# Recurrent pairs of an RWKV-7 block on one core: the state step as two 64x64 products instead of one block-diagonal 128x128 product

## The chip, the cores and the metric

The kernel runs on one core of one Trainium2 chip. The metric is the device time of one execution in microseconds (us). Matrix products run on TensorE (PE, its weight loads PEld), elementwise work on VectorE (DVE) and ScalarE (ACT), the low halves of the weights on GpSimd (POOL), and SyncE (SP) issues most transfers. All data is fp32; the sequence has 512 tokens, and the width is 1024.

## What is computed

The reference is a block that holds an RWKV-7 recurrence, dilated attention, a cross attention and an FFN, followed by two layers of another block (Fourier mixing, retention, convolutional FFN). Only the recurrence is touched. It has 16 heads, each with a state of 64 x 64:

```python
def step(state, inp):
    r_t, w_t, k_t, v_t, a_t, b_t = inp
    sa = jnp.einsum('bhij,bhj->bhi', state, a_t)
    state = state * w_t[:, :, None, :] + sa[..., None] * b_t[:, :, None, :] + v_t[..., None] * k_t[:, :, None, :]
    return state, jnp.einsum('bhij,bhj->bhi', state, r_t)
```

## The kernel before

**Layout.** The kernel does not step token by token. It cuts the 512 tokens into 8 chunks of 64 (`NC = 8`, `CH = 64`) and treats two heads at a time (`PAIRS = 8`): one head of a pair lies in partitions 0 to 63, the other in 64 to 127 (`HALVES`). Within a chunk everything is turned into small products, and from chunk to chunk a 64 x 64 state is carried per head: state(c+1) = decay x (map(c) applied to state(c)) + new part(c). The map of a chunk is the identity plus a 64 x 64 product, kept in `MCX`. In `MCX` each chunk has 128 columns: the upper head's 64 x 64 map in rows 0 to 63 and columns 0 to 63, the lower head's in rows 64 to 127 and columns 64 to 127, and zeros in the other two quarters. One product with all 128 rows then steps both heads.

**Order on PE.** The order is written out by hand in the body of `for p in range(PAIRS)`. Each pair issues some thirty groups of products (`to_tokens`, L1254; `to_heads`, L1265; both work on 64 x 64 quarters of the array, all four quarters in turn). Between them stand pieces of other matrix products (`pieces(n)`): one piece is one 128-row block of a projection and is three products of 128x512, L906, L907 and L910 (high x high, high x low, low x high). Near the end of a pair stand the groups `N` and `RM`, two pieces, then the scan:

```python
b = start_group("scan", p)
pe.wait_ge(sem("rw_mcx"), p + 1)
scan_step(b, 1)
pieces(1)
scan_step(b, 2)
```

and so on to `scan_step(b, 6)`, after which `values_inside` (L1298, L1301: quarter products in the two diagonal quarters) follows without a piece between. So a pair has six state steps, and five of them stand between two pieces. A state step is at L1435 (one product, 128x128 stationary `MCX[:, c, :]`, 64 moving columns); from the second on it waits for the state before it. An fp32 product of this kind, L1435 as L1298, shows as two MATMUL records and two weight loads; the transposes at L1273 as one.

**Order on DVE.** When `RM` is made, DVE writes the maps (`state_map`, L3066) once for each head, 64 partitions at a time, the second of which releases `rw_mcx`. Then it makes state 2 (`scanned(1)`, L3075), adds a term to x (L3147), and makes states 3 to 7, with work for the next pair in between (L2955, L2935, L2939). At the start of the kernel it clears `MCX` once (L2816).

Of the kernel before, what the change touches and what calls it, by code (L numbers as in the profile page):

```python
# [16 lines left out]
P = 128  # L17
F32 = mybir.dt.float32
F32R = mybir.dt.float32r
ALU = mybir.AluOpType  # L20
# [8 lines left out]
CH = 64  # L29
NC = S // CH  # L30
# [240 lines left out]
def build_program(nc, plan, ap, out):  # L271
# [4 lines left out]
    for t, T in enumerate(tiles):  # L276
        for i, (u, _, _) in enumerate(T["blocks"]):
            last_block[u] = (t, i)
# [12 lines left out]
    with ctx:  # L291
# [5 lines left out]
        def sem(name):  # L297
            if name not in sems:
                sems[name] = ctx.enter_context(nc.semaphore(name))
            return sems[name]  # L300
# [30 lines left out]
        def take(*shape):  # L331

            n = 1
            for x in shape:
                n *= x
            a = arena[:, free_at[0]:free_at[0] + n]
            free_at[0] += n
            assert free_at[0] <= ARENA, (free_at[0], ARENA)
            if len(shape) == 2:
                return a.rearrange("p (a b) -> p a b", b=shape[1])  # L340
            if len(shape) == 3:
                return a.rearrange("p (a b c) -> p a b c", b=shape[1], c=shape[2])
            return a

        def prm(name, j=0, n=1):
            return params[:, PCOL[name][0] + j:PCOL[name][0] + j + n]

        def tab(name):
            return table[:, TCOL[name][0]:TCOL[name][1]]

        ident, ones, heads, centring, strict, incl, ident_c, reset, quads = (
            tab(n) for n in ("ident", "ones", "heads", "centre", "strict", "incl", "ident_c", "reset", "quads"))
# [32 lines left out]
        main_arena = arena  # L385
        arena, free_at[0] = arena2, 0
        AR1 = take(NC, 2, CH)
        MCX = take(NC, P)
        BK, KK_, NP_, SC_ = (take(NC, CH) for _ in range(4))
        free_at[0] = 5 * KT * S // 4 + 3 * S  # L390
        YT, YSQ, BO1 = (take(S) for _ in range(3))
# [165 lines left out]
        def units_until(end):  # L557

            at = {}
            for j, t in enumerate(NOW[0] + NOW[1]):  # L560
                for i, (u, _, _) in enumerate(tiles[t]["blocks"]):
                    at[u] = KT * j + i
            return max([min(at)] + [u + RING for u in at if at[u] <= end])
# [55 lines left out]
        def emptied(eng, name, p):  # L619

            e, n = EMPTIED[name, p]
            eng.wait_ge(sem("rw_emptied_" + e), n)

        def made(eng, name, p):

            early = 1 if name == "aB" and p else 0
            late = 1 if name == "Y" and p + 1 < PAIRS else 0
            eng.wait_ge(sem("rw_made"), STEP_NO[name, p] + 1 - early + late)
# [5 lines left out]
        def in_columns(name, p, w):  # L634

            return slot_of(name, p)[:, :, 0:4 * w].rearrange("p b (d s) -> p b d s", s=w)
# [5 lines left out]
        def by_head(x):  # L642

            return x.rearrange("p (d r) s -> p r d s", r=2)

        HALVES = slice(0, CH), slice(CH, P)

        def state(c):

            return SC_[:, c, :] if c > 1 else NP_[:, 0, :]  # L650
# [23 lines left out]
        def rsqrt(n):  # L674

            return stats[:, n % 2, :]
# [103 lines left out]
        @block.sync  # L780
        def _(sp):
            first_up = min(u for u, _, _ in tiles[stages["up0"][0]]["blocks"])
            for u in range(n_units):
                n = u - first_up - 3 - ADA_LATE
# [79 lines left out]
        def _(pe):  # L864
# [377 lines left out]
            def start_group(name, p):  # L1242
                n = STEP_NO[name, p] - 2
                if n >= 0:
                    emptied(pe, *STEP_AT[n])
                return slot_of(name, p)
# [148 lines left out]
            for p in range(PAIRS):  # L1395
# [33 lines left out]
                def scan_step(b, c):  # L1429

                    if c == 1:
                        emptied(pe, "N", p)
                    else:
                        pe.wait_ge(sem("rw_state"), p * (NC - 3) + c - 1)
                    mm = nc.tensor.matmul(b[:, 0, CH * c:CH * (c + 1)], MCX[:, c, :], state(c), start=True, stop=True)  # L1435
                    mm.then_inc(sem("rw_made" if c == NC - 2 else "rw_stepped"), 1)

                if p == 0:
# [79 lines left out]
# [6 lines that stand above are left out]
                scan_step(b, 3)  # L1524
                pieces(1)
                scan_step(b, 4)
# [63 lines left out]
            for hd in range(XH):  # L1590
# [6 lines left out]
                for c in range(TC):  # L1597
                    for n, (k, (a, b)) in enumerate(itertools.product(range(2), HI_LO)):
                        mm = nc.tensor.matmul(banks[4 + c // 2][:, M * (c % 2):M * (c % 2 + 1)],
                                              XQS[a][:, (2 * hd + k) % 4, c * P:(c + 1) * P], KMS[b][:, 2 * hd + k, :],  # L1600
                                              start=(n == 0), stop=(n == 5))
# [13 lines left out]
                for m in range(2):  # L1615
                    for c in range(TC):
                        mm = nc.tensor.transpose(banks[6 + m][:, c * P:(c + 1) * P], XP[:, c, m * P:(m + 1) * P], ident)
# [6 lines left out]
                for d in range(2):  # L1624
                    for n, (m, (a, b)) in enumerate(itertools.product(range(2), HI_LO)):
                        mm = nc.tensor.matmul(banks[6 + d][:], VMS[a][:, m, 256 * hd + P * d:256 * hd + P * (d + 1)],
                                              XPTS[b][:, m, :], start=(n == 0), stop=(n == 5))
# [46 lines left out]
            for l in range(LAYERS):  # L1674
# [85 lines left out]
                for hd in range(XH):  # L1760
# [3 lines left out]
                    for c in range(TC):  # L1764
# [3 lines left out]
                        for k in range(2):  # L1768
# [3 lines left out]
                            mm = nc.tensor.matmul(o, RK_LO[:, k, cols], RQ_HI[:, k, :], start=False, stop=(k == 1))  # L1772
# [8 lines left out]
                    for d in range(2):  # L1781
                        for c in range(TC):
# [3 lines left out]
                            mm = nc.tensor.matmul(o, RV_LO[:, c, cols], high, start=False, stop=(c == TC - 1))  # L1786
# [7 lines left out]
                    for c in range(TC):  # L1794
                        mm = nc.tensor.matmul(banks[5][:, c:c + 1], ROT[:, 2, c * P:(c + 1) * P], ones[:, 0:1], start=True,
                                              stop=True)
# [24 lines left out]
            for c in range(TC // 2):  # L1821
                mm = nc.tensor.transpose(banks[6][:, c * P:(c + 1) * P],
                                         rsqrt(len(REQUESTS) - 1)[:, c:c + 1].to_broadcast([P, P]), ident)
# [741 lines left out]
        def _(dve):  # L2565
            counts = {}
            V_ = nc.vector

            def do(ins, signal="vector_step", value=None):

                if value is None:
                    value = counts[signal] = counts.get(signal, 0) + 1
                ins.then_inc(sem(signal), 1)
                dve.wait_ge(sem(signal), value)
# [238 lines left out]
            do(V_.tensor_scalar(half_k_a, prm("k_a", 0, KT), 0.5, None, ALU.mult))  # L2813
            do(V_.tensor_scalar(rest_k_a, half_k_a, -1.0, 1.0, ALU.mult, ALU.add))
            do(V_.tensor_scalar(half_bias, prm("w0", 0, 16), 0.5, None, ALU.mult), "rw_zeroed")
            do(V_.memset(MCX, 0.0))  # L2816

            def difference(t, i):
                evacuated(dve, t)
# [42 lines left out]
            for it in range(2 * TC):  # L2862
                m, c = it // TC, it % TC
# [29 lines left out]
            def mask(m):  # L2893
                return m.unsqueeze(1).unsqueeze(1).to_broadcast([P, 2, 4, CH])
# [140 lines left out]
            for p in range(PAIRS):  # L3035
# [26 lines left out]
                rm = in_columns("RM", p, P)  # L3062
                x = by_head(AR[:, :, 1, :])

                def state_map(r, signal="vector_step"):
                    do(V_.tensor_tensor(by_head(MCX[r, :, r]), rm[r, :, :, CH:P], mask(ident_c)[r], ALU.add), signal)  # L3066

                def scanned(c):

                    last = c == NC - 2  # L3070
                    if last:
                        made(dve, "scan", p)
                    else:
                        dve.wait_ge(sem("rw_stepped"), p * (NC - 3) + c)
                    do(V_.scalar_tensor_tensor(state(c + 1), slot_of("scan", p)[:, 0, CH * c:CH * (c + 1)],  # L3075
                                               w_end[:, c:c + 1], NP_[:, c, :], ALU.mult, ALU.add),
                       "rw_emptied_v" if last else "rw_state")
# [58 lines left out]
                if more:  # L3136
# [4 lines left out]
                                    w_end.rearrange("p (d r) -> p r d", r=2).unsqueeze(3).to_broadcast([P, 2, 4, CH]),  # L3141
                                    ALU.mult), "rw_emptied_v")
                made(dve, "RM", p)
                state_map(HALVES[0])
                state_map(HALVES[1], "rw_mcx")
                scanned(1)
                do(V_.tensor_tensor(x, x, rm[:, :, :, 0:CH], ALU.add), "rw_emptied_v")  # L3147
                scanned(2)
# [209 lines left out]
            for l in range(LAYERS):  # L3358
# [109 lines left out]
                rows = slice(64, 96)  # L3468
# [300 lines left out]
```

## Time and profile before

| | before |
|---|---|
| median of 3 runs | 2911.92 us (2911.47 to 2911.98) |
| the profiled execution | span 2909.9 us, of which the median lies 2.0 us above |
| PE busy | 2892.3 us, 99% of the span |
| DVE / ACT / POOL busy | 54% / 38% / 54% |
| state steps L1435 | 48 products (96 records), 241 to 563 us |
| map writes L3066 | 16 x 0.69 us |

The page gives no other time of the profiled execution than its span; the 2.0 us between the two lie around the span. The pairs run from about 206 to 565 us of the span. In the timelines the first column is the start of a row in us from the start of the span, the second its length, and xN is the number of records merged into the row. The start of one row to the start of the next is the time that PE spends on it; the lengths overlap.

### The profile page before, as it was taken

What the parts mean: (1) busy time and instruction counts of PE and PEld (TensorE: products, weight loads), DVE (VectorE), ACT (ScalarE), POOL (GpSimd) and SP (SyncE); (2) the same over time, 40 slices, a digit from 0 to 9 for tenths busy, and PEclk for the clock granted to TensorE, in tenths of its full rate; (3) what the DMA queues carried; (4) which work ended last, traced back from release to release, by engine and by line L of the source; (5) the groups of instructions that cost most, each with busy time, mean ns of one, the idle gap of its engine ahead of it and who ended that gap; (6) DMA issues with size and microseconds to landing.
All of it is one profiled execution on the core that took longest, in us unless ns stands there. A gap on an engine that the chain in (4) does not pass through costs nothing.

```text
span 2909.9 us, 49401 instructions
## 1 busy us (share of the span) xinstructions
PE 2892.3 (99%) x19658; PEld 2423.8 (83%) x19658; DVE 1572.7 (54%) x2227; ACT 1103.5 (38%) x1673; POOL 1584.3 (54%) x1912
## 2 busy tenths in 40 slices
PE   9999999999999999999999999999999999999998
PEld 7877777788888888888888898888898888988887
DVE  5467877524556666775334265445763441473635
ACT  4454434333443322443433343233443342342323
POOL 6432233355646666677444557565584444565654
PEclk9999999999999999999999999999999999999999
DMA  5211111332426777533222323232333222232232
GB/s 173 94 45 41 42 55 45 97 141 95 130 82 217 252 273 254 179 113 126 85 89 73 95 87 113 87 109 87 106 124 115 77 88 87 87 102 94 94 102 73
DMA packets 92292, 322.21 MB, mean 111 GB/s; under 512 B 10144, under 2 KB 14368, under 8 KB 91808
## 3 DMA queue, kind: packets, MB, share of 16 engines
q1 hardware_dynamic: 84544, 302.39, 31.7%
q10 hardware_dynamic: 7520, 16.67, 1.7%
q8 instruction: 156, 2.56, 0.4%
q14 instruction: 72, 0.59, 0.1%
HBM read 315.09 MB, written 3.93 MB: 110 GB/s over the span
## 4 chain that ended last, share of the span: by engine, by line
PE 98%; issue 1%; DVE 1%; POOL 1%; DMA 0%; ACT 0%; POOLq 0%; SPq 0%; ACTq 0%; DVEq 0%
PE bank L906 25%; PE bank L910 25%; PE bank L907 25%; PE bank L1254 2%; PE bank L899 2%; PE bank L901 2%; PE bank L900 2%; PE bank L1265 2%; PE bank L1273 1%; PE bank L934 1%; PE bank L936 1%; PE bank L935 1%; PE bank L958 1%; PE bank L960 1%; PE bank L1785 1%
## 5 line engine op out<-in xcount | busy, mean ns | idle before, releaser
L837 POOL TENSOR_TENSOR w_lo<-w_raw,w_hi 128x256 fp32r<-128x256 f32 x1736 | 1419.2, 852 | 986.9 <-ACT w_hi L1862 980.5
L906 PE MATMUL bank<-act,w_hi 128*128 128x512 f32 (+1 forms) x3464 | 1312.7, 379 | 4.7 <-POOL w_lo L837 2.6
L910 PE MATMUL bank<-act,w_lo 128*128 128x512 f32 (+1 forms) x3464 | 1292.4, 373 | 0.0
L907 PE MATMUL bank<-act,w_hi 128*128 128x512 f32 (+1 forms) x3464 | 1291.4, 373 | 0.0
L906 PEld LDWEIGHTS bank<-act,w_hi 128*128 128x128 f32 x3464 | 652.9, 188 | 126.1 <-issue 8.3
L910 PEld LDWEIGHTS bank<-act,w_lo 128*128 128x128 f32 x3464 | 652.6, 188 | 115.2
L907 PEld LDWEIGHTS bank<-act,w_hi 128*128 128x128 f32 x3464 | 653.4, 189 | 106.7
L1862 ACT CAST w_hi<-w_raw 128x1024 fp32r<-128x1024 f32 (+1 forms) x438 | 454.4, 1043 | 345.1 <-DMA w_raw<-in_weights 163.6
L1870 ACT ACTIVATE arena<-bank 128x512 f32<-128x512 f32 (+1 forms) x177 | 104.3, 593 | 418.2 <-PE bank L910 401.6
L855 POOL TENSOR_TENSOR stats<-stats,exponent 128x8 f32<-128x8 f32 (+2 forms) x38 | 46.6, 1226 | 302.5 <-DVE stats L2914 150.0
L2600 DVE TENSOR_TENSOR act<-tmp,act 128x512 fp32r<-128x512 f32 (+1 forms) x140 | 121.2, 866 | 77.3 <-ACT act L1889 72.7
L3588 DVE TENSOR_SCALAR arena<-arena,params 128x512 f32<-128x512 f32 x88 | 53.0, 602 | 172.3 <-ACT arena L1870 171.9
L3323 DVE SCALAR_TENSOR_TENSOR arena<-arena,small 128x1024 f32<-128x1024 f32 x93 | 136.5, 1468 | 3.3
L837 POOL TENSOR_TENSOR w_lo<-arena,w_hi 128x256 fp32r<-128x256 f32 x128 | 114.9, 932 | 22.5 <-ACT w_hi L1862 22.5
L1889 ACT CAST act<-tmp 128x512 fp32r<-128x512 f32 (+1 forms) x140 | 84.4, 605 | 112.5 <-DVE tmp L3212 32.0
L2773 DVE SCALAR_TENSOR_TENSOR arena<-bank,small,arena 128x512 f32<-128x512 f32 x48 | 36.1, 751 | 166.9 <-PE bank L910 166.6
L2125 ACT ACTIVATE arena<-bank 128x512 f32<-128x512 f32 (+1 forms) x104 | 64.8, 631 | 114.3 <-PE bank L1273 96.9
L899 PE MATMUL bank<-w_hi,act 128*128 128x512 f32 (+1 forms) x224 | 84.5, 377 | 0.0
L3591 DVE SCALAR_TENSOR_TENSOR arena<-arena,params 128x512 f32<-128x512 f32 x88 | 82.6, 939 | 3.1
L901 PE MATMUL bank<-w_hi,act 128*128 128x512 f32 (+1 forms) x224 | 83.7, 374 | 0.0
L900 PE MATMUL bank<-w_lo,act 128*128 128x512 f32 (+1 forms) x224 | 83.7, 374 | 0.0
L2771 DVE TENSOR_TENSOR arena<-arena,bank 128x512 f32<-128x512 f32 x44 | 30.3, 688 | 89.5 <-PE bank L910 89.2
(359 smaller groups left out, 3087.4 us busy)
## 6 DMA issues: line engine op xcount, KB each, us to landing
w_raw<-in_weights SPq DMA_DIRECT2D x471, 512.0 KB, 3.5
arena<-in_ada SPq DMA_DIRECT2D x96, 512.0 KB, 5.0
arena<-in_strips ACTq DMA_DIRECT2D x8, 448.0 KB, 3.7
arena<-in_x ACTq DMA_DIRECT2D x1, 2048.0 KB, 10.9
y_scratch<-tmp ACTq DMA_DIRECT2D x7, 256.0 KB, 2.0
arena<-y_scratch ACTq DMA_DIRECT2D x1, 1792.0 KB, 8.1
arena<-in_dft ACTq DMA_DIRECT2D x2, 777.5 KB, 4.2
arena<-in_x SPq DMA_DIRECT2D x3, 512.0 KB, 7.4
```

Source lines behind the costliest of these rows:

```text
L837: ins = nc.gpsimd.tensor_tensor(w_lo[:, k, cols], weights_of(u)[:, cols], w_hi[:, k, cols].bitcast(F32), ALU.subtract)
L899: nc.tensor.matmul(o, xs[0], wh, start=first, stop=False)
L900: nc.tensor.matmul(o, xs[0], wl, start=False, stop=False)
L901: mm = nc.tensor.matmul(o, xs[1], wh, start=False, stop=last)
L906: nc.tensor.matmul(o, wh, xh, start=first, stop=False)
L907: nc.tensor.matmul(o, wh, xl, start=False, stop=False)
L910: mm = nc.tensor.matmul(o, wl, xh, start=False, stop=last)
L1862: nc.scalar.copy(x, y).then_inc(sem("w_high"), 1)
L1870: nc.scalar.activation(dst, banks[bank_of(t)][:, 0:n], func, scale=scale).then_inc(sem(f"bank_free{bank_of(t)}"), 1)
L1889: ins = nc.scalar.copy(o, x) if shift is None else nc.scalar.activation(o, x, ACT.Identity, bias=shift)
L2600: do(V_.tensor_tensor(o, x, h, ALU.subtract), "low_done")
L3323: do(V_.scalar_tensor_tensor(o, w, c_act[:, k:k + 1], o, ALU.mult, ALU.add), "ada_used")
```

## The change

`MCX` keeps only the two 64 x 64 maps, one above the other (64 columns to a chunk; the other half of the space is left unused, so that nothing behind it moves). A state step becomes two products, each 64 x 64 with 64 moving columns: rows 0 to 63 into output partitions 0 to 63, rows 64 to 127 into output partitions 64 to 127. DVE writes both maps with one operation over 128 partitions instead of two over 64, and the clearing at the start goes.

```diff
-        MCX = take(NC, P)
+        MCX = take(NC, CH)
+        take(NC * CH)
...
-                    mm = nc.tensor.matmul(b[:, 0, CH * c:CH * (c + 1)], MCX[:, c, :], state(c), start=True, stop=True)
+                    for rows in HALVES:
+                        mm = nc.tensor.matmul(b[rows, 0, CH * c:CH * (c + 1)], MCX[rows, c, :], state(c)[rows], start=True,
+                                              stop=True)
                     mm.then_inc(sem("rw_made" if c == NC - 2 else "rw_stepped"), 1)
...
-            do(V_.memset(MCX, 0.0))
...
-                def state_map(r, signal="vector_step"):
-                    do(V_.tensor_tensor(by_head(MCX[r, :, r]), rm[r, :, :, CH:P], mask(ident_c)[r], ALU.add), signal)
+                def state_map():
+                    do(V_.tensor_tensor(by_head(MCX), rm[:, :, :, CH:P], mask(ident_c), ALU.add), "rw_mcx")
...
-                state_map(HALVES[0])
-                state_map(HALVES[1], "rw_mcx")
+                state_map()
```

Line numbers shift by one or two in the changed kernel (L906, L907, L910 are L907, L908, L911 there, L1435 is L1437, L3066 is L3068).

On PE, at the last two state steps of the first pair, before the change:

```order
1357 L910 MATMUL bank<-act,w_lo 128x512
1358 L1435 MATMUL bank<-arena 128x64
1359 L906 MATMUL bank<-act,w_hi 128x512
1360 L907 MATMUL bank<-act,w_hi 128x512
1361 L910 MATMUL bank<-act,w_lo 128x512
1362 L1435 MATMUL bank<-arena 128x64
1363 L1298 MATMUL bank<-arena 64x64 x2
```

and now:

```order
1357 L911 MATMUL bank<-act,w_lo 128x512
1358 L1437 MATMUL bank<-arena 64x64 x2
1359 L907 MATMUL bank<-act,w_hi 128x512
1360 L908 MATMUL bank<-act,w_hi 128x512
1361 L911 MATMUL bank<-act,w_lo 128x512
1362 L1437 MATMUL bank<-arena 64x64 x2
1363 L1299 MATMUL bank<-arena 64x64 x2
```

The place of the step between the pieces is the same; one whole-array product has become two quarter products.

On DVE, where the first pair's maps are written, before the change:

```order
141 L3140 TENSOR_TENSOR arena<-bank,small 128x2x4x64
142 L3066 TENSOR_TENSOR arena<-bank,table 64x2x4x64 x2
143 L3075 SCALAR_TENSOR_TENSOR arena<-bank,small,arena 128x64
144 L3147 TENSOR_TENSOR arena<-arena,bank 128x2x4x64
145 L3075 SCALAR_TENSOR_TENSOR arena<-bank,small,arena 128x64
```

and now:

```order
140 L3142 TENSOR_TENSOR arena<-bank,small 128x2x4x64
141 L3068 TENSOR_TENSOR arena<-bank,table 128x2x4x64
142 L3077 SCALAR_TENSOR_TENSOR arena<-bank,small,arena 128x64
143 L3148 TENSOR_TENSOR arena<-arena,bank 128x2x4x64
144 L3077 SCALAR_TENSOR_TENSOR arena<-bank,small,arena 128x64
```

Two operations over 64 partitions have become one over 128, and nothing else on DVE changes its place.

## Rows read from the trace of the kernel before

**Rows 1.** The page: busy time of each engine, and the chain that ended last.

```profile
PE 2892.3 (99%) x19658; PEld 2423.8 (83%) x19658; DVE 1572.7 (54%) x2227; ACT 1103.5 (38%) x1673; POOL 1584.3 (54%) x1912
...
PE 98%; issue 1%; DVE 1%; POOL 1%; DMA 0%; ACT 0%; POOLq 0%; SPq 0%; ACTq 0%; DVEq 0%
```

**Rows 2.** Windows: stretch, its length, busy us of PE, PEld, DVE, ACT, POOL, clock.

```profile
284.97:290.60 5.63, 5.58 (x33) 4.16 (x33) 4.06 (x11) 0.00 (x0) 0.97 (x2) 1.00 0.47 160
557.29:562.90 5.61, 5.56 (x33) 4.16 (x33) 2.44 (x7) 0.00 (x0) 2.91 (x5) 1.00 0.59 184
565.00:1200.00 635.00, 635.00 (x3014) 532.53 (x3015) 347.49 (x427) 228.01 (x330) 387.05 (x455) 1.00 0.54 183
```

**Rows 3.** Timeline of PE, second pair: first, second and sixth state step.

```profile
284.97 0.40 PE L910 MATMUL bank<-act,w_lo 128*128 128x512 f32 x1
285.42 0.41 PE L1435 MATMUL bank<-arena 128*128 128x64 f32 x2
285.63 0.48 PE L906 MATMUL bank<-act,w_hi 128*128 128x512 f32 x1
285.95 0.40 PE L907 MATMUL bank<-act,w_hi 128*128 128x512 f32 x1
286.18 0.40 PE L910 MATMUL bank<-act,w_lo 128*128 128x512 f32 x1
286.42 0.33 PE L1435 MATMUL bank<-arena 128*128 128x64 f32 x2
286.56 0.48 PE L906 MATMUL bank<-act,w_hi 128*128 128x512 f32 x1
286.87 0.39 PE L907 MATMUL bank<-act,w_hi 128*128 128x512 f32 x1
...
290.18 0.33 PE L1435 MATMUL bank<-arena 128*128 128x64 f32 x2
290.44 0.33 PE L1298 MATMUL bank<-arena 64*64 64x64 f32 x4
290.60 0.28 PE L1301 MATMUL bank<-arena 64*64 64x64 f32 x4
290.72 0.28 PE L1298 MATMUL bank<-arena 64*64 64x64 f32 x4
```

**Rows 4.** Timeline of PE: a group on quarters between two pieces.

```profile
258.96 0.40 PE L910 MATMUL bank<-act,w_lo 128*128 128x512 f32 x1
259.29 0.69 PE L1265 MATMUL bank<-arena 64*64 64x64 f32 x32
259.92 0.50 PE L906 MATMUL bank<-act,w_hi 128*128 128x512 f32 x1
260.25 0.40 PE L907 MATMUL bank<-act,w_hi 128*128 128x512 f32 x1
```

**Rows 5.** Waits of PE's weight loads: us in total, times, longest.

```profile
PEld bank L1435 <- issue: 3.7, 8, 0.5
PEld bank L1435 <- DVE arena L3075: 2.6, 10, 0.4
```

**Rows 6.** Timeline of DVE, second pair, around its scan.

```profile
283.91 1.41 DVE L3066 TENSOR_TENSOR arena<-bank,table 64x512 f32<-64x512 f32 x2 [0.18 <-PE bank L1265]
...
285.93 0.28 DVE L3075 SCALAR_TENSOR_TENSOR arena<-bank,small,arena 128x64 f32<-128x64 f32 x1 [0.61 <-PE bank L1435]
286.25 0.69 DVE L3147 TENSOR_TENSOR arena<-arena,bank 128x512 f32<-128x512 f32 x1
...
290.01 0.69 DVE L2939 SCALAR_TENSOR_TENSOR arena<-arena 128x512 f32<-128x512 f32 x1
...
290.74 0.28 DVE L3075 SCALAR_TENSOR_TENSOR arena<-bank,small,arena 128x64 f32<-128x64 f32 x1
```

**Rows 7.** Timeline of DVE: the clearing at the start, and what follows it.

```profile
51.47 0.91 DVE L2816 MEMSET arena<- 128x1024 f32 x1 [0.28 <-DVE small L2815]
68.67 1.89 DVE L2874 SCALAR_TENSOR_TENSOR arena<-arena,bank 128x128 f32<-128x128 f32 x6 [16.28 <-PE bank L1182]
```

## The prediction

> **What bounds the kernel now.** The page comes first: PE is busy for 99% of the span, and 98% of the chain that ended last is PE [rows 1]. So a change counts by what it does to the time between PE's instructions, and work taken from DVE counts only where PE waits for it. The windows come next: behind the pairs lie 635 us in which PE has no gap at all [rows 2], so what the pairs gain or lose is not absorbed there. Then the timeline of PE at the state steps, because the change sits there, and the waits of its weight loads. I read starts, not lengths: a row's length holds the way through the array, which overlaps with the next row.
>
> **A state step now.** Take the second one of the pair [rows 3]: L910 to L1435 0.24 us, L1435 to L906 0.14, L906 to L907 0.31, L907 to L910 0.23 (285.95 to 286.18). That is 0.92 us for a step and a piece. A piece alone costs three times 0.23, 0.69, so an undisturbed step costs 0.23. Six steps, five with a piece, and the way into the quarter products (0.24, then 290.18 to 290.44, then to 290.60: 0.26 and 0.16) make 5 x 0.92 + 0.66 = 5.26 us. The window from the L910 before the first step to the first L1301 is 5.63 us in this pair and 5.61 in the last [rows 2]; the missing 0.37 are waits. At the first step PE comes 0.45 behind L910 instead of 0.24, and the next row 0.21 instead of 0.14 behind it: 0.28 us. The rest, 0.09, is at steps that wait for the state before them. Over the eight pairs the waits view shows both: 8 waits before the first step and 10 for L3075 [rows 5]. It names the first kind "issue", but DVE says what it is: the two map writes take until 285.32, and the load starts right behind [rows 6].
>
> **What the change does on DVE.** One write over 128 partitions instead of two over 64. An operation on 128x512 that also reads a bank, L3147, takes 0.69 us, and the two 64x512 writes take 1.41 together [rows 6]: length goes by the elements in a partition, so one write costs 0.69. The maps are ready at 283.91 + 0.69 = 284.60, before PE even starts the L910 at 284.97, so the wait at the first step goes in all eight pairs. The later waits go too: DVE is 0.7 us earlier, and PE comes later (below). Gain: 0.37 us in a pair, 3.0 in all. The clearing (0.91 us) is followed by 16.28 us of idle DVE [rows 7]; it was hidden by that and brings nothing.
>
> **What it does on PE.** The step becomes a small group on quarters of the array between two whole-array pieces. The trace has such groups, only larger [rows 4]:
> - L910 to the first quarter record: 0.33 us, against 0.24 to a whole-array step. The load does not run ahead beside L910.
> - first quarter record to the next L906: 0.63 for 32 records whose last one ends 0.69 after the start; so L906 starts 0.06 before the end of the group. For two products (4 records) in the two diagonal quarters, behind a whole-array product, the row at 290.44 is exactly the case: 0.33 long [rows 3]. So 0.33 - 0.06 = 0.27, against 0.14.
> - L906 to L907: 0.33 (259.92 to 260.25), against 0.31; I take 0.33 to 0.34. L907 to L910: 0.23 as before.
>
> Sum: 0.33 + 0.27 + 0.34 + 0.23 = 1.17 us for a step and a piece, 0.25 more than 0.92. The sixth step is followed by quarters anyway: 0.33 in, then 0.16 to L1298 (the gap behind a first pair of products), then 0.12 as from 290.60 to 290.72: 0.61 against 0.66. A pair thus needs 5 x 1.17 + 0.61 = 6.46 us against 5.63, +0.83, of which the waits that go are already taken off. Eight pairs: +6.6 us. On the profiled span that is 2909.9 to 2916.5; on the median, which is 2.0 above it, 2918.5.
>
> The unknown is the gap of 0.27. Its lower bound is the whole-array step's own 0.14 (then a pair's sum is 0.65 less, +1.4 us in all), its upper bound the 0.63 of the large group (+21 us). I stay near 0.27 because the row of 0.33 has the same four records; the 0.63 holds eight times as many.
>
> Here a rule of the Trainium skill bears on the case. In "TensorEngine Tiling (Array Packing)", Key Properties, it says that changing the tiling mode, and not only the tile, drains TensorE; it speaks against this change, which adds ten such changes to a pair, and the trace agrees with 0.33 against 0.24. The same page's Theoretical Speedup promises up to twice the rate where a dimension is 64 or less; by that alone the 48 steps would cost half of 0.23 each and the sum would be a gain of 5.5 us, 8.5 with the waits. Which of the two decides hangs on how many products share one change of mode: sixteen in the groups of the trace, two here.
>
> **What is late next.** DVE starts a state 0.10 after its product ends (285.83 to 285.93) [rows 3, 6]. With a step every 1.17 us, the next product is made 1.17 later, while DVE needs 0.28 for the state, 0.69 for the longest work between (L2939) and some 0.1 of gaps: 1.1 us. So no new wait for the state, with 0.1 to spare. At the sixth step DVE then starts 0.33 + 0.10 behind it, 0.15 behind the first L1301, where it is 0.14 now: what follows keeps its distance.
>
> **Rivals.**
> - *Price of leaving the quarters is hidden* (not slower). L906's weights are loaded while the four small records run, as they are behind a whole-array step: gaps 0.33, 0.16, 0.31, 0.23 = 1.03. A pair is 5 x 1.03 + 0.61 = 5.76, +0.13, in all +1 us: 2913. For it: a pair leaves half of the array untouched, and four records are few. Against it: each quarter group that is followed by a piece has L906 to L907 at 0.33, which shows the load uncovered. It decides if the gap behind a pair is under 0.2.
> - *No price for the change of mode at all* (faster). Gaps 0.23, 0.12, 0.23, 0.23 = 0.81; with the sixth step at 0.23 + 0.12 + 0.12 a pair takes 4.5, -1.1, in all -9 us: 2903. The rule of the speedup in the Trainium skill (same page) would have it so. Against it: no quarter group between pieces in the trace shows 0.23 on its way in.
> - *The two products don't run side by side* (slower still). If L906 has to wait for two pair gaps rather than one, 0.12 more a step: 40 x 0.12 = 4.8 on top, 2923. For it: an isolated pair has no later products to fill the array. Against it: the row of 0.33 is already the whole pair.
> - *The order on PE hides another wait.* That DVE's 0.7 us come back elsewhere would give at most 5.6 us; against it, DVE's next state is tied to PE's step, so DVE cannot run ahead. I count it with the first rival.
>
> **How the numbers follow.** A measurement of this kernel can tell about 0.2%, 5.8 us, from no change. Forecast, both changes of mode paid: 0.70, with its own range of +4.5 to +9 us, three quarters of it above 5.8. Price of leaving hidden, with little lost or gained: 0.14. No price: 0.06. Not side by side: 0.10. Slower by over 0.2%: 0.54 + 0.10 = 0.64; within: 0.16 + 0.14 = 0.30; faster: 0.06. The range reaches from the first rival to the third, and leaves out the fast case and the tails: 2912.5 to 2923.0.
>
> **What the profile after should show.** L1437 with 192 records on 64*64; the wait "issue" before it gone as a wait for DVE, though a gap behind L911 may bear that name; DVE L3068 eight times at 0.69; from L911 to L1437 0.33 at every step, the first like the others; from L1437 to L907 0.27; from L907 to L908 0.34; the window from the L911 before the first step to the first L1302 at 6.46 us in every pair; 635 us of a PE without gaps unchanged behind. I am wrong if that window is under 6.2 or over 6.8 us, or if PE's gaps change outside the eight windows.

## The result, and the profile after

The changed kernel takes 2918.41 us in the median of 12 runs (2917.88 to 2920.05), the kernel before, beside it, 2911.85 us (2911.47 to 2912.72). The ratio is 1.0023, with an interval from 1.0016 to 1.0030: slower by 6.6 us, where 2918.5 was forecast. The profiled execution has a span of 2916.5 us, against 2909.9.

The page of the changed kernel, busy time by engine, answers to [rows 1]:

```profile
PE 2897.9 (99%) x19754; PEld 2418.5 (83%) x19754; DVE 1565.4 (54%) x2218; ACT 1103.5 (38%) x1673; POOL 1578.6 (54%) x1912
```

PE is busy for 5.6 us longer and has 96 records more (48 steps with four instead of two). Its weight loads are busy for less time: a load of 64 columns takes 0.13 us instead of 0.19, and the loads of the two quarters overlap. DVE has nine instructions and 7.3 us less. Neither saving of busy time shortens the span by itself, because the span follows the starts of PE's products; what the earlier maps save is measured below (two_writes).

The window that the sum was made for, from the L911 before the first step to the first L1302, of the second and of the last pair (same columns as [rows 2]):

```profile
285.67:292.06 6.39, 6.39 (x45) 3.69 (x45) 3.80 (x10) 0.00 (x0) 0.96 (x2) 1.00 0.37 126
562.75:569.12 6.37, 6.37 (x46) 3.69 (x46) 2.10 (x6) 0.00 (x0) 2.92 (x5) 1.00 0.49 167
```

6.39 us instead of 5.63, and PE is busy for all of it. The eight windows add up to 51.17 us, against 45.25 before. The timeline of PE in the second pair, to be laid beside [rows 3]:

```profile
285.67 0.39 PE L911 MATMUL bank<-act,w_lo 128*128 128x512 f32 x1
285.99 0.33 PE L1437 MATMUL bank<-arena 64*64 64x64 f32 x4
286.25 0.50 PE L907 MATMUL bank<-act,w_hi 128*128 128x512 f32 x1
286.58 0.39 PE L908 MATMUL bank<-act,w_hi 128*128 128x512 f32 x1
286.81 0.40 PE L911 MATMUL bank<-act,w_lo 128*128 128x512 f32 x1
287.14 0.33 PE L1437 MATMUL bank<-arena 64*64 64x64 f32 x4
287.40 0.50 PE L907 MATMUL bank<-act,w_hi 128*128 128x512 f32 x1
287.74 0.39 PE L908 MATMUL bank<-act,w_hi 128*128 128x512 f32 x1
...
291.78 0.33 PE L1437 MATMUL bank<-arena 64*64 64x64 f32 x4
291.94 0.28 PE L1299 MATMUL bank<-arena 64*64 64x64 f32 x4
292.06 0.28 PE L1302 MATMUL bank<-arena 64*64 64x64 f32 x4
```

From L911 to the step 0.32 to 0.33 us, to the next L907 0.26, to L908 0.33 to 0.34, to L911 0.23: 1.15 to 1.16 us for a step and a piece, at the first step as at the others. The sixth step takes 0.16 to L1299.

The waits view of the changed kernel, between 180 and 600 us, names something that the prediction had ruled out:

```profile
PEld bank L1437 <- DVE arena L3077: 14.6, 40, 0.4
...
PEld bank L1437 <- issue: 2.9, 8, 0.4
```

L3077 is the state step on DVE. Read at face value, 40 of the 48 steps wait for the state before them, 14.6 us in all, five times what stood there before [rows 5]. DVE's timeline, though, has the state done early (second pair):

```profile
284.60 0.69 DVE L3068 TENSOR_TENSOR arena<-bank,table 128x512 f32<-128x512 f32 x1 [0.18 <-PE bank L1266]
286.43 0.28 DVE L3077 SCALAR_TENSOR_TENSOR arena<-bank,small,arena 128x64 f32<-128x64 f32 x1 [1.14 <-PE bank L1437]
```

The maps are ready at 285.29, before the L911 at 285.67; state 2 is ready at 286.71, before the L911 at 286.81, and the step comes at 287.14. Whether the waits view or this reading is right is the first question for the experiments.

### The profile page after: what moved, and what is told of

Read it like the earlier page. It is cut to its first block, busy times and chain, and to the rows that moved or that the text cites. A ratio compares the mean times of both kernels' runs of the same rounds, so it can differ in the third digit from the quotient of the medians.

```text
span 2916.5 us, 49584 instructions
## 1 busy us (share of the span) xinstructions
PE 2897.9 (99%) x19754; PEld 2418.5 (83%) x19754; DVE 1565.4 (54%) x2218; ACT 1103.5 (38%) x1673; POOL 1578.6 (54%) x1912
## 4 chain that ended last, share of the span: by engine, by line
PE 97%; issue 1%; POOL 1%; DVE 1%; DMA 0%; ACT 0%; POOLq 0%; SPq 0%; ACTq 0%; DVEq 0%
PE bank L907 26%; PE bank L908 25%; PE bank L911 25%; PE bank L1255 2%; PE bank L900 2%; PE bank L902 2%; PE bank L901 2%; PE bank L1266 2%; PE bank L1274 1%; PE bank L935 1%; PE bank L937 1%; PE bank L936 1%; PE bank L959 1%; PE bank L961 1%; PE bank L1788 1%
## 5 line engine op out<-in xcount | busy, mean ns | idle before, releaser
L907 PE MATMUL bank<-act,w_hi 128*128 128x512 f32 (+1 forms) x3464 | 1313.1, 379 | 5.1 <-POOL w_lo L838 2.8
L911 PE MATMUL bank<-act,w_lo 128*128 128x512 f32 (+1 forms) x3464 | 1291.9, 373 | 0.0
L908 PE MATMUL bank<-act,w_hi 128*128 128x512 f32 (+1 forms) x3464 | 1290.9, 373 | 0.4 <-issue 0.4
L907 PEld LDWEIGHTS bank<-act,w_hi 128*128 128x128 f32 x3464 | 652.2, 188 | 130.0 <-issue 8.9
L911 PEld LDWEIGHTS bank<-act,w_lo 128*128 128x128 f32 x3464 | 652.2, 188 | 116.2 <-issue 0.6
L908 PEld LDWEIGHTS bank<-act,w_hi 128*128 128x128 f32 x3464 | 652.8, 188 | 106.2
```

The lines of the kernel that those rows point to most:

```text
L907: nc.tensor.matmul(o, wh, xh, start=first, stop=False)
L908: nc.tensor.matmul(o, wh, xl, start=False, stop=False)
L911: mm = nc.tensor.matmul(o, wl, xh, start=False, stop=last)
```

## The experiments

All runs are against the kernel before on the same chip. "Window" is the stretch of the second pair as above (from the row ahead of its first step to the first row of the second line of `values_inside`), "sum" that of all eight pairs, both taken from starts in the timeline of the one profiled execution.

| kernel | window | sum | median us | before, same chip |
|---|---|---|---|---|
| before | 5.63 | 45.25 | | 2911.8 to 2912.1 |
| after | 6.39 | 51.17 | 2918.41 | 2911.85 |
| one_write | 5.33 | 42.67 | 2909.18 | 2911.81 |
| two_writes | 6.52 | 52.10 | 2918.76 | 2911.81 |
| free_state | 6.41 | 51.12 | 2918.86 | 2911.81 |
| doubled | 7.09 | 56.63 | 2923.58 | 2911.81 |
| one_product | 6.26 | 50.08 | 2917.59 | 2912.01 |
| column_halves | 6.66 | 53.32 | 2919.82 | 2912.01 |
| six_maps | 5.37 | 42.90 | 2909.74 | 2912.01 |
| six_maps_mixed | 5.52 | 44.26 | 2911.28 | 2912.01 |
| halved_sum | 5.32 | 42.97 | 2909.95 | 2911.91 |
| halved_sum_mixed | 5.26 | 42.57 | 2909.69 | 2911.91 |
| third_piece | 5.33 | 42.66 | 2912.36 | 2912.14 |

Median less sum lies between 2866.5 and 2867.7 us for all but third_piece (2869.7), which moves work out of the window. So the medians follow the windows within some 1 us, and what is said of differences under 1 us rests on the windows. The 95% intervals of the ratios reach about 0.1%, some 2.6 us, to either side. The medians of the kernels that come out 2 to 2.6 us under the kernel before are therefore not clear of no change by these intervals; that they save rests on the windows, and on times that don't overlap with those before (one_write 2908.69 to 2909.49 against 2911.36 to 2913.18; halved_sum's times do overlap).

**Each part by itself: one_write and two_writes.** The first keeps the whole-array step and writes the maps with one operation:

```diff
-                state_map(HALVES[0])
-                state_map(HALVES[1], "rw_mcx")
+                do(V_.tensor_tensor(by_head(MCX[:, :, 0:CH]), rm[:, :, :, CH:P], mask(ident_c), ALU.add), "rw_mcx")
```

> The whole-array step of the kernel before, but both maps written by one operation over 128 partitions into columns 0 to 63 of MCX, so that the lower head's map stands in the wrong columns (its state is not the reference's); only the DVE part of the change. Theory (the change = waits removed, -3.0 us, plus two changes of tiling mode at each isolated step, +9.1 us): this run shows the first term alone. Window from the L910 before the first step to the first L1301 5.26 to 5.30 us instead of 5.63, span 2.6 to 3.0 us under before. Rival (DVE is in lockstep with PE and the earlier maps bring nothing, the wait only moves to the next step): window 5.6, span unchanged. Second rival (the clock or the waits elsewhere carry the difference): the window changes, but the span by another amount than eight times it.

Measured: window 5.33 instead of 5.63, median 2.6 us under before. The first term stands, though 0.52 of the 2.58 us of the sum come from the seventh pair alone, which was longer than the others before (last section). The 0.03 to 0.07 us more than expected are one wait that stays: the third step's, one in each pair:

```profile
PEld bank L1435 <- DVE arena L3075: 2.0, 8, 0.3
```

The addition to x (0.69 us) stands between DVE's first and second state and makes the second late. I had thought that DVE's lead would carry over; it doesn't, since DVE's first state waits for PE's first step.

The second writes the maps twice, on 64 partitions each, in the changed kernel:

```diff
-                def state_map():
-                    do(V_.tensor_tensor(by_head(MCX), rm[:, :, :, CH:P], mask(ident_c), ALU.add), "rw_mcx")
+                def state_map(r, signal="vector_step"):
+                    do(V_.tensor_tensor(by_head(MCX[r]), rm[r, :, :, CH:P], mask(ident_c)[r], ALU.add), signal)
```

> The changed kernel with the two 64-partition map writes of before: only the PE part of the change, the output is the same. Theory: the steps cost what they cost in the changed kernel (1.155 us for a step and a piece), and the first step waits for the maps again, but little, since on quarters PE comes only 0.33 behind L911 in any case and the second write ends 0.35 behind it: 0.1 us a pair, so 0.8 to 1.0 us over the changed kernel. With one_write this makes the parts add up: after - before = +6.6 = (-3) + (+9.5). Rival (the maps' wait costs as much as before, 0.28): 2.3 us over the changed kernel.

Measured: window 6.52, 0.13 more than the changed kernel, 0.9 us over the eight pairs as expected; the median shows 0.35 of it. So the one write is worth 0.30 us a pair to whole-array steps and 0.12 to quarter steps (0.93 over eight pairs). Taken alone, the PE part costs 52.10 - 45.25 = 6.9 us, and the DVE part gives back 0.9 of it. The two parts don't add: most of the wait that the DVE part removes would have been hidden behind the drain that the PE part brings.

**Is it the state that PE waits for: free_state.**

```diff
-                    else:
-                        pe.wait_ge(sem("rw_state"), p * (NC - 3) + c - 1)
...
-                        mm = nc.tensor.matmul(b[rows, 0, CH * c:CH * (c + 1)], MCX[rows, c, :], state(c)[rows], start=True,
+                        mm = nc.tensor.matmul(b[rows, 0, CH * c:CH * (c + 1)], MCX[rows, c, :], NP_[rows, 0, :], start=True,
...
-                    do(V_.scalar_tensor_tensor(state(c + 1), slot_of("scan", p)[:, 0, CH * c:CH * (c + 1)],
+                    do(V_.scalar_tensor_tensor(state(c + 1), NP_[:, c, :],
```

> The changed kernel with the recurrence cut: every step reads NP_[:, 0] instead of the state before it and doesn't wait for it, and DVE makes its states from NP_ alone and not from the scan's bank (the recurrence is left out, the output is not the reference's). The number and the place of all instructions stay. Rival (the waits view of the changed kernel is right: 40 waits of PE's weight loads for L3077, 14.6 us): the span falls by up to 14.6 us. Theory (DVE had the state 0.1 us before L911 even started; what lies between L911 and the step is the change of tiling mode, and the view puts it down to the semaphore that came last): no change of the span beyond 0.5 us, step and piece still 1.155 us, L911 to the step still 0.33.

Measured: 2918.86 us, sum of the windows 51.12 against 51.17. No step waits for a state any more, and nothing is gained. The waits view of this run (the step is L1435 here):

```profile
PEld bank L1435 <- issue: 17.4, 48, 0.4
```

17.4 us at 48 steps, where the changed kernel has 14.6 + 2.9 = 17.5 at 40 + 8. The gap is the same to 0.1 us; only its name has changed. It belongs to the change of tiling mode, not to the state. The view puts a gap down to the last semaphore event ahead of it, and that was DVE's state, which had come 0.1 us before L911 even began.

**What the price hangs on: doubled and one_product.** `for rows in HALVES` becomes `for rows in HALVES * 2` in the one, and in the other

```diff
-                    for rows in HALVES:
+                    for rows in HALVES[:1]:
```

> The changed kernel with each step's two products issued twice, to the same place: 8 records instead of 4. Theory (a fixed price for going into the quarters and back, and 0.12 us for each pair of products within): a step and a piece 1.27 us instead of 1.155, 48 x 0.12 = 5.6 us over the changed kernel. Rival (isolated products on quarters don't overlap, and each pays its own way through the array): 0.2 us or more for each pair of products, 10 us or more over the changed kernel. Rival (the products are free beside the change of mode): under 2 us.

> The changed kernel with only the upper head's product in each step (the lower head's recurrence is left out, its states come from what the bank holds). 2 records instead of 4. Doubling the products cost 0.114 us a pair of products. Theory (side by side: the two products run in two quarters at once, and what takes 0.11 is the two passes of each, one after the other in its quarter): leaving one product out saves nothing, a step and a piece 1.15 us, under 0.6 us in all. Rival (in order: each product takes 0.057 whatever its quarter): a step and a piece 1.10 us, 48 x 0.057 = 2.7 us under the changed kernel. In both the price of going in and out, some 0.3 us, stays; if that went with the product (a step under 1.0 us), the change of mode would not be what costs.

Measured, second pair, doubled first:

```profile
286.23 0.40 PE L911 MATMUL bank<-act,w_lo 128*128 128x512 f32 x1
286.56 0.45 PE L1437 MATMUL bank<-arena 64*64 64x64 f32 x8
286.94 0.50 PE L907 MATMUL bank<-act,w_hi 128*128 128x512 f32 x1
287.27 0.40 PE L908 MATMUL bank<-act,w_hi 128*128 128x512 f32 x1
```

and one_product:

```profile
285.81 0.40 PE L911 MATMUL bank<-act,w_lo 128*128 128x512 f32 x1
286.13 0.33 PE L1437 MATMUL bank<-arena 64*64 64x64 f32 x2
286.39 0.50 PE L907 MATMUL bank<-act,w_hi 128*128 128x512 f32 x1
...
291.90 0.27 PE L1437 MATMUL bank<-arena 64*64 64x64 f32 x1
291.91 0.27 PE L1299 MATMUL bank<-arena 64*64 64x64 f32 x1
```

The way in (0.32 to 0.33) and the way out to L908 (0.33) are the same in both. From the step to L907 it is 0.38 us with four products, 0.26 with two and 0.26 with one. So a second pair costs 0.12 us (5.2 us in the median over the changed kernel), and the second product of the first pair costs nothing at an isolated step: the two quarters do work at once. Record by record the trace says the same: in the changed kernel the four records of the first step start at 285.986, 285.992, 286.092 and 286.098, and the two of one_product 0.107 us apart. So the second product starts 0.006 us behind the first, beside it, and only the second record of each has to wait for its first. The saving of one_product, 0.8 us in the median and 1.1 in the sum, is more than the 0.6 that were expected at most. Nearly all of it comes from the sixth step, where its last rows show L1299 starting 0.01 us behind it, beside it in the array, and not 0.16. The side-by-side theory holds, and with it the rival of a pair that doesn't run side by side is out.

**Is it the cut by rows: column_halves.** The kernel before, with the step cut by columns only:

```diff
-                    mm = nc.tensor.matmul(b[:, 0, CH * c:CH * (c + 1)], MCX[:, c, :], state(c), start=True, stop=True)
+                    for rows in HALVES:
+                        mm = nc.tensor.matmul(b[rows, 0, CH * c:CH * (c + 1)], MCX[:, c, rows], state(c), start=True, stop=True)
```

> The kernel before (block-diagonal MCX, two map writes) with each step as two products that use all 128 rows and one half of the columns each, so that the array is cut by columns only; the output is the same. Theory (any change of the tiling costs, whatever the shape): a step and a piece 1.155 us, and one more change behind the sixth step, where PE goes from column halves to quarters: window 6.5 to 6.75 us, some 8 to 9 us over before. Rival (what costs is the cut by rows, which takes away the loads that run ahead): 0.24 into the step, a step and a piece under 1.05 us, under 4 us over before.

```profile
287.10 0.40 PE L910 MATMUL bank<-act,w_lo 128*128 128x512 f32 x1
287.43 0.34 PE L1436 MATMUL bank<-arena 128*64 128x64 f32 x4
287.69 0.50 PE L906 MATMUL bank<-act,w_hi 128*128 128x512 f32 x1
288.03 0.39 PE L907 MATMUL bank<-act,w_hi 128*128 128x512 f32 x1
...
292.05 0.34 PE L1436 MATMUL bank<-arena 128*64 128x64 f32 x4
292.32 0.33 PE L1298 MATMUL bank<-arena 64*64 64x64 f32 x4
```

0.33, 0.26, 0.34: the price of the quarters, for a cut that keeps all 128 rows. Behind the sixth step, where PE goes from column halves to quarters, it takes 0.27 (292.05 to 292.32) where the changed kernel takes 0.16, so this change costs too. Window 6.66, inside the forecast; the median, 7.8 us over before, is just under the 8 to 9 expected.

**Keeping the gain without the price.** As the gain lies on DVE, I tried to have it with whole-array steps. Only chunks 1 to 6 are ever used as maps, and in `RM`'s two banks they are one contiguous stretch:

```diff
+                used = slot_of("RM", p).rearrange("p b n -> p (b n)")[:, P:7 * P].rearrange("p (k j s) -> p k j s", k=2, s=P)
+                maps = MCX[:, 0:6, :].rearrange("p (k j) s -> p k j s", k=2)
...
-                    do(V_.tensor_tensor(by_head(MCX[r, :, r]), rm[r, :, :, CH:P], mask(ident_c)[r], ALU.add), signal)
+                    do(V_.tensor_tensor(maps[r, :, :, r], used[r, :, :, CH:P], mask(ident_c)[r, :, 0:3], ALU.add), signal)
```

(`scan_step` reads `MCX[:, 3 + c // 2]` for odd c and `MCX[:, c // 2 - 1]` for even c.)

> The kernel before, whole-array steps, but DVE writes only the six maps that the steps use (chunks 1 to 6) and not eight: two operations on 64x384 instead of 64x512. 64 elements take 0.28 us, 256 take 0.42 and 512 take 0.69, so 384 should take 0.56: the maps are ready 0.26 us earlier in each pair. Theory: of the 0.28 us of the first step's wait 0.2 to 0.28 go, the later waits stay: window 5.35 to 5.43 us instead of 5.63, median 1.6 to 2.2 us under before. Rival (the write has a fixed length or the wait moves on): window 5.6.

```profile
283.68 1.15 DVE L3072 TENSOR_TENSOR arena<-bank,table 64x384 f32<-64x384 f32 x2 [0.19 <-PE bank L1265]
```

1.15 us for both writes instead of 1.41, window 5.37, median 2.3 us under before (ratio 0.9992, interval 0.9983 to 1.0001). The window is as expected; the median is just beyond the 1.6 to 2.2 us, since the seventh pair gave 0.49.

> As six_maps, and two edits more: DVE adds to x (L3147 in the kernel before) behind the second state and not behind the first, so that the second state is not kept waiting; and only the sixth step, which stands in front of products on quarters anyway, is done as two quarter products (out of the 128-column MCX). Theory: no waits in the scan, 5 x 0.92 + 0.61 = 5.21 us, with up to 0.07 of waits left: window 5.21 to 5.28 instead of 5.63, 2.8 to 3.4 us under before, at or under the one-write run (2909.2), and the only one of these whose output is the reference's and that beats both kernels. Rival (x is needed for something behind the scan and its move gives the gain back as a wait there): the window falls, the span by less than 2 us.

The two edits on top of six_maps:

```diff
+                    if c == NC - 2:
+                        for rows in HALVES:
+                            mm = nc.tensor.matmul(b[rows, 0, CH * c:CH * (c + 1)], MCX[rows, map_of(c), rows],
+                                                  state(c)[rows], start=True, stop=True)
...
                 scanned(1)
-                do(V_.tensor_tensor(x, x, rm[:, :, :, 0:CH], ALU.add), "rw_emptied_v")
                 scanned(2)
+                do(V_.tensor_tensor(x, x, rm[:, :, :, 0:CH], ALU.add), "rw_emptied_v")
```

A miss: 5.52 us and 2911.28. The wait had only moved, and grown:

```profile
287.65 0.40 PE L910 MATMUL bank<-act,w_lo 128*128 128x512 f32 x1
288.06 0.43 PE L1443 MATMUL bank<-arena 128*128 128x64 f32 x2
```

```profile
286.80 0.69 DVE L3159 TENSOR_TENSOR arena<-arena,bank 128x512 f32<-128x512 f32 x1
287.51 0.17 DVE L2963 COPY small<-arena 128x8 f32<-128x8 f32 x1
287.72 0.28 DVE L3086 SCALAR_TENSOR_TENSOR arena<-bank,small,arena 128x64 f32<-128x64 f32 x1
```

Behind the second state already stood the copy of 0.17 us; with the addition that is 0.86 us in a slot of about 0.5, and the fourth step comes 0.41 behind L910 instead of 0.24. The last pair, which has no copy there, took 5.32. I had counted the edit and not its new neighbour.

The next two cut the addition in halves of 256 elements, one behind each of the first two states, without and with the sixth step on quarters:

> As six_maps (whole-array steps, six maps written), and DVE's addition to x cut into two halves of 256 elements, one behind the first state, one behind the second. In six_maps_mixed the whole addition (0.69 us) with the copy of 0.17 behind the second state made the fourth step wait 0.17 and more. Theory (between two states DVE has 0.92 - 0.28 - some 0.1 = 0.54 us free): a half of 0.42 fits behind the first state; behind the second 0.42 + 0.17 is about 0.05 too long or just fits. Window 5.28 to 5.33 us instead of 5.36 in six_maps, median 0.2 to 0.6 us under six_maps (2909.7). Rival (the operation's fixed part makes two halves dearer than one whole, and a later state waits): window 5.4 or more.

> As halved_sum, and the sixth step as two quarter products in front of the products on quarters. Theory (a group that is followed by quarters anyway pays no way back): 0.05 us a pair less than halved_sum, 0.4 us in all, window 5.23 to 5.28 us. Rival (the sixth step on quarters comes 0.08 later than on the whole array, DVE's seventh state with it, and PE waits for it behind values_inside): the window falls, the span doesn't.

Windows 5.32 and 5.26, as expected, so the sixth step on quarters gains 0.05 to 0.06 us where quarters follow. The sums are another matter for halved_sum: 42.97 against 42.90 in six_maps, because its seventh pair took 5.86 (last section). Medians 2909.95 and 2909.69, with six_maps at 2909.74: the three cannot be told apart (halved_sum_mixed has a long seventh pair too, 5.81), and halved_sum missed the 0.2 to 0.6 us under six_maps that was expected of it.

**More cover instead of less work: third_piece.** `pieces(2)` ahead of the scan becomes `pieces(3)`.

> The kernel before, whole-array steps, with three pieces of other products in front of the first state step instead of two (the third is taken from the end of the same pair, behind values_of_states); DVE is unchanged, so nothing is computed otherwise. Theory (the first step's wait is only that DVE's two map writes end 0.2 us too late): the wait of 0.28 us goes, window 5.35 us instead of 5.63, as in six_maps. What it does to the span depends on the end of the pair: PE then comes 0.3 us later to the scan and has one piece less as cover for DVE's queue behind it. Either the covers there are long enough and the median is 2.2 us under before (2909.7), or PE waits for DVE at the start of the next pair (0.36 us at the turned triangle already now) and gets most of it back: 0 to 3 us over before. I take the second for likelier, since DVE has no idle time between its seventh state and the next pair.

Window 5.33, and a median of 2912.36 against 2912.14. Here the gain is given back at the start of the next pair:

```profile
294.37 0.39 PE L910 MATMUL bank<-act,w_lo 128*128 128x512 f32 x1
295.13 1.10 PE L1254 MATMUL bank<-arena 64*64 64x128 f32 x32 [0.38 <-ACT arena L2125]
```

The group of the next pair comes 0.76 behind the last piece, where the way into quarters is otherwise 0.33. Not DVE, as I had expected, but ACT is the releaser there: the place was right, the engine not.

## Why the prediction was right, step by step

- **The bound.** Right: what PE's starts lost in the windows is in the median, within some 1 us. Of 7.3 us less of DVE 0.9 us reached the windows, where PE waited for the maps (two_writes); 5.3 us less of weight loads show in none.
- **Way in 0.33, way out 0.27, next load 0.34.** Measured 0.33, 0.26, 0.33 to 0.34. The estimate of 0.27 from the row of the same four records [rows 3] was good to 0.01, and its two ends, 0.14 and 0.63, were never near. A step and a piece takes 1.157 instead of the 1.17 of the sum (285.67 to 291.45 for five), and the sixth step 0.61 as forecast; that makes 6.39 instead of 6.46.
- **The maps' wait.** Gone in all pairs, as said. But its worth depends on what stands beside it: 0.30 on whole-array steps, 0.12 on quarters (one_write, two_writes). The sum was right, because it set whole windows against each other; "+9.5 and -3.0" as two independent terms would have been wrong, and the expectation of two_writes still wrote it so.
- **Waits for the state.** In the changed kernel they are gone, as free_state shows. The reason given, DVE being 0.7 us earlier, was half wrong: in one_write DVE is as early, and the third step still waits. They go because PE comes 0.23 us later to every step.
- **The total.** The eight windows grew by 5.9 us, not 6.6: 0.5 us less because of the 6.39, and 0.2 because the forecast took 5.63 us for every pair before, while the seventh took 5.86 (last section). The other 0.6 to 0.7 us lie outside, where I had said that nothing would change, so one of the forecast's own signs of being wrong came true. In the profiled execution PE stood still twice, once within a piece (0.43 us, "issue", at 421.46, two records ahead of the fifth pair's first step) and once at L1620 for DVE (0.55 us, at 787.06); a wait of 0.39 us that stood at 548.10 before (L1254) is gone. The stop at L1620 shows in free_state, doubled and one_product as well, 0.55 us each, and in no other kernel, so it isn't a matter of one execution; what brings it about stays open, as it does for the other. So the agreement to 0.1 us is partly luck: the windows 0.7 us under the sum, and as much over it elsewhere.
- **The rivals.** "The way out is hidden" fell to the 0.26 and 0.34; "no price" to the 0.33; "not side by side" fell to one_product and to the starts of the records. The speedup that the Trainium skill gives in "TensorEngine Tiling (Array Packing)", Theoretical Speedup, did not show: a step costs 0.47 us on top of its piece (1.157 less 0.69), where the whole-array step cost 0.23. What it says of a drain at a change of tiling mode (Key Properties) agrees with the 0.33 on the way in and the 0.26 on the way out.

## What to carry to other kernels

Before a product is split into smaller ones on parts of the array, count the changes of tiling, not the elements: here a group of one, two or four small fp32 products between whole-array products costs 0.23 us or more on top of what the whole-array product with its zero quarters cost, and only groups that already stand beside others of the same tiling are cheap (the sixth step gained 0.05). A block-diagonal operand padded with zeros is then the cheaper form, and if its writing is what PE waits for, shorten the writing: six maps instead of eight gave a third of what the change cost, with the other sign. And a wait that a view pins on a semaphore is only a guess: look whether the named engine was done before, or take the dependency out and see if the gap stays.

## What was not expected of the hardware

**A cut by columns alone costs as much as one by rows and columns.** 128 rows by 64 columns behaved like 64 by 64 to 0.01 us. A cut by rows alone was not run.

**Some DVE operations take longer in a stretch in which POOL works without a break.** In the seventh pair of the kernel before, the window took 5.86 us instead of 5.63. PE waits there for states that come late, and DVE's timeline shows why:

```profile
508.78 0.28 DVE L3075 SCALAR_TENSOR_TENSOR arena<-bank,small,arena 128x64 f32<-128x64 f32 x1
509.10 0.78 DVE L2955 COPY small<-arena 128x8 f32<-128x8 f32 x1
509.91 0.28 DVE L3075 SCALAR_TENSOR_TENSOR arena<-bank,small,arena 128x64 f32<-128x64 f32 x1
510.23 0.59 DVE L2935 SCALAR_TENSOR_TENSOR arena<-arena 128x256 f32<-128x256 f32 x1
```

The copy takes 0.78 us instead of 0.17 and the 128x256 operation 0.59 instead of 0.42, while the states, which read a bank, stay at 0.28. Over the same stretch POOL is busy all the time (kernel before):

```profile
506.34 7.09 POOL L837 TENSOR_TENSOR w_lo<-w_raw,w_hi 128x256 fp32r<-128x256 f32 x9
```

In the second pair it works for 0.97 us of 5.63. The page "SBUF — State Buffer" of the Trainium skill, section "SBUF: two separate sides", says that VectorE and GpSimd share a pair of ports under an exclusive lock, which DVE operations in a two-port mode need, or with two inputs in SBUF against a GpSimd operation that reads SBUF. The trace fits it: the long ones have their inputs in SBUF, as has POOL's L837. No run here was made to test it, but free_state happens to bear on it. There the same states read no bank, and in its seventh pair, while POOL is busy, four of the six take 0.53 to 0.71 us:

```profile
513.18 0.53 DVE L3075 SCALAR_TENSOR_TENSOR arena<-arena,small 128x64 f32<-128x64 f32 x1
514.38 0.71 DVE L3075 SCALAR_TENSOR_TENSOR arena<-arena,small 128x64 f32<-128x64 f32 x1
```

In its second pair, where POOL is idle from 286.6 us on, all take 0.28 us. The quarter steps of the changed kernel, with their longer period, hid the long operations (6.39 us in that pair too, though its L2937 took 0.63 and its L2941 1.10 us there); halved_sum did not (5.86), and lost there what it had gained in the other seven. The period alone doesn't decide it. The kernels six_maps, one_write and third_piece, with steps as close together as in the kernel before, took 5.33 to 5.37 us in the seventh pair: their copy took 0.35 to 0.38 us and the 128x256 operations behind it 0.42 to 0.45, with POOL as busy. Which operations are hit differs from kernel to kernel, and no run here shows what decides it.
